# Experts placed by their row count with a capacity per place; gate and up with the weights held still

## What is computed

```python
eidx, gates = _route(xt, router_w, router_bias)      # 6 of 64 experts for each row, and their weights
...
def step(acc, blk):                                  # a block: rows tok of one expert e, gates g
    tok, g, e = blk
    xb = xpad[tok]
    hid = jax.nn.silu(xb @ w_gate[e]) * (xb @ w_up[e])   # (rows, 1024) @ (1024, 256), twice
    yb = (hid @ w_down[e]) * g[:, None]                  # (rows, 256) @ (256, 1024)
    return acc.at[tok].add(yb.astype(acc.dtype)), None
```

## Time and profile before

| what | value |
|---|---|
| median of 3 runs | 2303.5 us (2300.52 to 2303.54) |
| the profiled execution, its own time | 2310.06 us |
| its span in the trace | 2307.7 us |
| TensorE, busy share of the span | 94% |
| VectorE, ScalarE, GpSimd | 61%, 49%, 28% |
| granted TensorE clock, mean | 0.97 |
| first and last matmul of the experts stage | 1028.4 us and 2236.0 us |

### The profile page before, as it was taken

One profiled execution on the slowest core, in us unless ns is written; L12 is line 12 of the kernel. 1 busy time (PEld: TensorE's weight loads), 2 busy tenths in 40 slices (PEclk: granted clock), 3 DMA queues, 4 the chain that ended last, 5 costly groups with the idle time before them and its releaser, 6 DMA issues. The chain is left out here.

```text
span 2307.7 us, 34429 instructions
## 1 busy us (share of the span) xinstructions
PE 2164.2 (94%) x10800; PEld 1766.7 (77%) x10800; DVE 1405.2 (61%) x2590; ACT 1129.7 (49%) x1866; POOL 645.4 (28%) x597
## 2 busy tenths in 40 slices
PE   6999999999899999959999999999999999999970
PEld 5777778777678888747888888888888888888850
DVE  5444444444677877746666666666666666666638
ACT  4344334433533333215556565555655565655537
POOL 1111111111113233332333333333333333333310
PEclk9999999999899999969999999999999999999995
DMA  6101101012623323247999989999999998999958
GB/s 218 40 31 34 41 32 37 34 41 84 244 67 107 101 81 109 93 161 224 284 286 279 277 275 285 281 280 281 280 287 284 284 278 276 275 286 280 282 110 323
DMA packets 194561, 435.84 MB, mean 189 GB/s; under 512 B 35488, under 2 KB 40080, under 8 KB 193200
## 3 DMA queue, kind: packets, MB, share of 16 engines
q1 hardware_dynamic: 150928, 289.49, 36.8%
q0 software_dynamic: 43312, 144.90, 23.6%
q10 hardware_dynamic: 288, 1.05, 0.1%
HBM read 328.16 MB, written 109.39 MB: 190 GB/s over the span
## 5 line engine op out<-in xcount | busy, mean ns | idle before, releaser
L1706 PE MATMUL ex_psU<-ex_guh,ex_xh 128*128 128x512 f32 x1024 | 413.8, 404 | 3.7 <-DVE ex_xl L1691 3.7
L1708 PE MATMUL ex_psU<-ex_guh,ex_xl 128*128 128x512 f32 x1024 | 402.6, 393 | 0.0
L1707 PE MATMUL ex_psU<-ex_gul,ex_xh 128*128 128x512 f32 x1024 | 400.5, 391 | 0.0
L1555 POOL DMA_INDIRECT acc_d<-ex_y,ex_use x128 | 206.3, 1612 | 410.1 <-ACT ex_y L1618 348.9
L1708 PEld LDWEIGHTS ex_psU<-ex_guh,ex_xl 128*128 128x128 f32 x1024 | 193.1, 189 | 43.3
L1706 PEld LDWEIGHTS ex_psU<-ex_guh,ex_xh 128*128 128x128 f32 x1024 | 193.3, 189 | 40.7 <-DVE ex_xl L1691 4.3
L1707 PEld LDWEIGHTS ex_psU<-ex_gul,ex_xh 128*128 128x128 f32 x1024 | 193.9, 189 | 37.5
L1577 POOL DMA_INDIRECT ex_xg<-h_d,entries x128 | 199.3, 1557 | 59.2 <-issue 38.1
L1706 PE MATMUL ex_psY<-ex_dnh,ex_hdh 128*128 128x512 f32 x512 | 210.2, 411 | 1.7 <-DVE ex_hdl L1662 1.7
L1618 ACT ACTIVATE ex_y<-ex_psY 128x1024 f32<-128x1024 f32 x128 | 131.3, 1025 | 143.3 <-PE ex_psY L1708 143.3
L1708 PE MATMUL ex_psY<-ex_dnh,ex_hdl 128*128 128x512 f32 x512 | 200.0, 391 | 0.0
(11 more groups left out here) (351 smaller groups left out, 4400.1 us busy)
## 6 DMA issues: line engine op xcount, KB each, us to landing
mi_g_raw<-w_experts SPq DMA_DIRECT2D x96, 1024.0 KB, 11.8
mi_g_place<-w_experts SPq DMA_DIRECT2D x96, 1024.0 KB, 11.8
mi_xr<-xT SPq DMA_DIRECT2D x17, 512.0 KB, 3.5
acc_d<-de_acc SPq DMA_DIRECT2D x17, 512.0 KB, 13.3
h_d<-de_h POOLq DMA_DIRECT2D x17, 512.0 KB
ln_t<-acc_d SPq DMA_DIRECT2D x17, 512.0 KB, 5.8
y<-ln_t SPq DMA_DIRECT2D x17, 512.0 KB, 4.4
de_cr<-cat SPq DMA_DIRECT2D x16, 512.0 KB
```

What stands on the lines that cost most here:

```text
L1555: nc.gpsimd.indirect_dma_start(out=io["acc_d"], out_offset=bass.IndirectOffsetOnAxis(ap=use[:, k, 0:1].bitcast(U32), axis=0), in_=y[:, k, ...
L1706: nc.tensor.matmul(out, lh, rh, start=start, stop=False)
L1707: nc.tensor.matmul(out, lh, rl, start=False, stop=False)
L1708: return nc.tensor.matmul(out, ll, rh, start=False, stop=stop)
```

## The change

1. **Ranks.** At the end of the dense stage the experts get places: experts 0 and 1 keep the first two, the other 62 follow in rising order of their number of rows. This takes one comparison of all counts with all counts, an inverse by a matmul, and two more round trips between TensorE and VectorE. The order stands in `ov`; SyncE reads the expert of each place from there.
2. **Capacities.** A place has its own number of rows n: 256 for the first two, then 10 places of 176, 14 of 192, 10 of 208, 10 of 220, 8 of 236, 10 of 256 (`CLASSES`). An expert with more rows than its place has the rest in further blocks of 256, which still go in pairs after all others. Each class is a hardware loop of its own with its first pair (on GpSimd two) written out. The second tile of a place has n - 128 rows in gather, add, rounding, split and output.
3. **Gate and up.** The weights are held still (128 x 128 blocks, 32 per expert and part) and the rows move. High and low part of the rows lie side by side in `xs`, so the high weight block meets both in one matmul of 2n columns, and the low weight block meets the high rows in one of n columns. The two halves of the result are added: ScalarE copies the second half (`lo`), VectorE adds (`sums`). The result is hidden x rows, as `down` needs it: `hidden_T`, `psH` and their work are gone. The gate of the rows is now the scale of the output copy.
4. **Order.** A step is now an expert: second half of gate/up of e-1, transposes of tile 0 of e, `down` of tile 0 of e-2, transposes of tile 1, `down` of tile 1, first half of gate/up of e. The adds of e-3 stand behind the gathers of e (before: e-2). The weight transfers wait for their own third of `raw[b]` alone, and a partition's part of a transfer is one piece of 8 KB (before four of 2 KB).

The core of the diff:

```diff
+CLASSES = ((1, 6, 176), (6, 13, 192), (13, 18, 208), (18, 23, 220), (23, 27, 236), (27, 32, 256))
+CAPS = [BLK] * 2 + [n for begin, end, n in CLASSES for _ in range(2 * (end - begin))]
...
-            sp.wait_ge(S["blocks_dve"], 3)
+            sp.wait_ge(S["blocks_dve"], 5)
...
-        xh, y = sb("xh", [P, 2, KC, P], F32R), sb("y", [P, 4, D])
+        xs, hdh = sb("xs", [P, KC, 2, BLK], F32R), sb("hdh", [P, 2, FC, BLK], F32R)
+        lo, gu0 = sb("lo", [P, 2, BLK]), sb("gu0", [P, 2, BLK])
-        psX, psU = ps("psX", [P, D]), ps("psU", [P, 2, 2 * FF])
-        psH, psY = ps("psH", [P, FC * P]), ps("psY", [P, D])
+        psX, psU, psY = ps("psX", [P, D]), ps("psU", [P, FC, 2, 2 * BLK]), ps("psY", [P, 2, D // 2])
...
+            pair(0, BLK, BLK, None)
+            before = BLK
+            for begin, end, n in CLASSES:
+                for p in range(begin, begin + peeled):
+                    pair(p, before, n, None)
+                    before = n
+                with eng.Fori(begin + peeled, end) as p:
+                    pair(p, n, n, None)
...
-                    hold(sp, s_split, 12 * p + 6 * b - 6, s_sp_passed)
                     for kind in range(3):
-                        w = io["w_experts"][bass.ds(e, 1), kind].rearrange("o k p n -> (o p) k n")
+                        hold(sp, s_split, 12 * p + 6 * b - 10 + 2 * kind, s_sp_passed)
+                        w = io["w_experts"][bass.ds(e, 1), kind].rearrange("o p n -> (o p) n")
...
+            # ScalarE
+            def pair(p, n1, n, j):
+                for b in range(2):
+                    e, m = 2 * p + b, n if b else n1
+                    copy_lo(e - 1, 0, m)
+                    round_w(p, e, b, (0,))
+                    sigmoid(e - 1, 0, m)
+                    round_w(p, e, b, (1,))
+                    hidden(e - 1, 0, 1 - b, m)
+                    round_w(p, e, b, (2,))
+                    copy_lo(e - 1, 1, m)
+                    round_x(e, 0, n)
+                    sigmoid(e - 1, 1, m)
+                    round_w(p, e, b, (3,))
+                    output(e - 2, b, (0, 1), n1)
+                    round_x(e, 1, n)
+                    hidden(e - 1, 1, 1 - b, m)
+                    output(e - 2, b, (2,), n1)
+                    round_w(p, e, b, (4,))
+                    output(e - 2, b, (3,), n1)
+                    round_w(p, e, b, (5,))
...
+            # VectorE
+                    sums(e - 1, 0, m)
+                    split_w(e, b, (0,))
+                    activate(e - 1, 0, m)
+                    split_w(e, b, (1,))
+                    hidden(e - 1, 0, 1 - b, m)
+                    sums(e - 1, 1, m)
+                    split_x(e, 0, n)
+                    activate(e - 1, 1, m)
+                    split_w(e, b, (2,))
+                    split_x(e, 1, n)
+                    split_w(e, b, (3,))
+                    hidden(e - 1, 1, 1 - b, m)
+                    split_w(e, b, (4, 5))
...
+            def transpose_x(p, e, b, t):
+                pe.wait_ge(s_row[2 * b + t], 16 * (p + 1))
+                after(pe, s_xl, 2 * e + t)
...
+            def gate_up(e, b, f, n):
+                if f == 0:
+                    pe.wait_ge(s_xl, 2 * e + 2)
+                after(pe, s_sum, 2 * e + f - 1)
+                for half in range(2):
+                    c0 = half * FF + f * P
+                    for kc in range(KC):
...
+                        nc.tensor.matmul(psU[:, f, half, 0:2 * n].rearrange("p (s n) -> p s n", s=2), guh[:, b, kc, c0:c0 + P],
+                                         xs[:, kc, :, 0:n], start=(kc == 0), stop=False)
+                        last = nc.tensor.matmul(psU[:, f, half, 0:n], gul[:, b, kc, c0:c0 + P], xs[:, kc, 0, 0:n],
+                                                start=False, stop=(kc == KC - 1))
...
+            def pair(p, n1, n, j):
+                for b in range(2):
+                    e = 2 * p + b
+                    gate_up(e - 1, 1 - b, 1, n if b else n1)
+                    for t in range(2):
+                        transpose_x(p, e, b, t)
+                        down(e - 2, b, t, n1)
+                    gate_up(e, b, 0, n)
```

More of the change, by code:

```diff
@@ L1238, in _ @@
             V.memset(oneb[:], 1.0)
+            V.memset(onesq[:], 1.0)
             V.memset(macc[:], 0.0)
@@ L1505, in piece, with pairs @@
             return src, dnh[:, b, part, :], dnl[:, b, part, :]
[L1507 to L1513, removed]
+        def pairs(eng, pair, peeled=1):
+            more = eng.value_load(ov[0:1, MORE:MORE + 1], min_val=0, max_val=OVP)
+            pair(0, BLK, BLK, None)
[6 more added lines that the diff above has]
+                    pair(p, n, n, None)
             with eng.If(more > 0):
@@ L1580, in pair @@
[L1580 to L1589 removed]
+                            out=xg[0:r, k, :], out_offset=None, in_=io["h_d"],
@@ new lines, in _, with copy_lo, sigmoid @@
+            A = nc.scalar.activation
+            def copy_lo(e, f, n):
+                if exists(e):
+                    act.wait_ge(s_gu, 2 * e + f + 1)
+                    after(act, s_hid, 2 * e + f)
+                    A(lo[:, :, 0:n], psU[:, f, :, n:2 * n], ACT.Copy).then_inc(s_lo, 1)
+            def sigmoid(e, f, n):
+                if exists(e):
+                    act.wait_ge(s_sum, 2 * e + f + 1)
+                    A(lo[:, 0, 0:n], gu[f][:, 0, 0:n], ACT.Sigmoid).then_inc(s_sig, 1)
@@ L1656, in _ @@
+            e = 2 * pairs(act, pair)
+            copy_lo(e - 1, 0, BLK)
+            sigmoid(e - 1, 0, BLK)
+            hidden(e - 1, 0, 1, BLK)
+            copy_lo(e - 1, 1, BLK)
+            sigmoid(e - 1, 1, BLK)
+            output(e - 2, 0, range(2), BLK)
+            hidden(e - 1, 1, 1, BLK)
+            output(e - 2, 0, range(2, 4), BLK)
+            output(e - 1, 1, range(4), BLK)
         @block.vector
@@ L1701, in _ @@
+            e = 2 * pairs(dve, pair)
+            for f in range(FC):
+                sums(e - 1, f, BLK)
+                activate(e - 1, f, BLK)
+                hidden(e - 1, f, 1, BLK)
         @block.tensor
@@ L1728, in down @@
-            def down(m, b, pieces):
-                pe.wait_ge(s_hl, m + 1)
-                pe.wait_ge(s_split, pieces)
-                pe.wait_ge(s_y, m)
-                for hf in range(2):
-                    cols = slice(hf * 512, (hf + 1) * 512)
+            def transpose_x(p, e, b, t):
+                pe.wait_ge(s_row[2 * b + t], 16 * (p + 1))
+                after(pe, s_xl, 2 * e + t)
+                for kc in range(KC):
+                    last = nc.tensor.transpose(psX[:, kc * P:(kc + 1) * P], xg[:, 2 * b + t, kc * P:(kc + 1) * P], ident[:])
+                last.then_inc(s_xT, 1)
@@ L1734, in down @@
+            def down(e, b, t, n):
+                if not exists(e):
+                    return
+                pe.wait_ge(s_hl, 2 * e + 2)
+                pe.wait_ge(s_split, 6 * e + 6)
+                r = rows_of(n, t)
+                for half in range(2):
+                    u = 2 * t + half
+                    after(pe, s_y, 4 * e + u - 1)
                     for f in range(FC):
-                        last = three(psY[:, cols], hdh[:, f, :], hdl[:, f, :], dnh[:, b, f, cols], dnl[:, b, f, cols],
+                        last = three(psY[0:r, half, :], hdh[:, b, f, t * P:t * P + r], hdl[:, b, f, t * P:t * P + r],
+                                     dnh[:, b, f, half * 512:(half + 1) * 512], dnl[:, b, f, half * 512:(half + 1) * 512],
@@ L1760, in _, with pair @@
-            end = pairs(pe, pair)
-            n = 4 * end
-            hidden_T(n - 2, 2)
-            gate_up(n - 1, 3, 1, 12 * end - 2)
-            down(n - 2, 1, 12 * end)
-            hidden_T(n - 1, 3)
-            down(n - 1, 1, 12 * end)
+                    last.then_inc(s_dn, 1)
+            def pair(p, n1, n, j):
+                for b in range(2):
+                    e = 2 * p + b
+                    gate_up(e - 1, 1 - b, 1, n if b else n1)
+                    for t in range(2):
+                        transpose_x(p, e, b, t)
+                        down(e - 2, b, t, n1)
+                    gate_up(e, b, 0, n)
@@ L1770, in stage_norm @@
+            e = 2 * pairs(pe, pair)
+            gate_up(e - 1, 1, 1, BLK)
+            for t in range(2):
+                down(e - 2, 0, t, BLK)
+            for t in range(2):
+                down(e - 1, 1, t, BLK)
 def stage_norm(nc, io):
```

319 lines of the change are left out of this document (139 added, 180 removed).

## The result

The changed kernel takes 2498.8 us (median of 4 runs, 2494.8 to 2500.0) against 2302.6 in the same comparison: 1.085 of the time, 95% interval 1.083 to 1.087. The forecast was 2219 us, faster; the kernel is 196 us slower, and outside the range.

The account below looks back on a forecast made before the run. TensorE was taken as the bound: its expert stretch falls from 1207.6 to 1117.7 us (-90), +4.3 behind it and +1 at the start give -84.6, so 2303.5 becomes 2219 us; range 2190 to 2262.

Parts of the forecast that it names:

- Transfers: Weights, rows, entries and gathers per expert: 4.90 MB in a mean 17.2 us, POOL's extra copy hidden, cost 0.
- the other side: Gate/up rival: short float32r matmuls run like plain float32, 150 to 500 us more, 2370 to 2720 us; chance 0.07.
- my 0.117 us: Gate/up: price of each n-column matmul for all n, between 0.109 for 128-column transposes and 0.1235 for 256 columns.
- the first rival: Gate/up: short matmuls cost their columns alone, the load hides fully; 25 us less, 2194 us; chance 0.10.
- its 0.109: Spacing in us of 128-column transposes in the earlier trace, used as evidence that the block load's time shows.
- the narrow cover of 0.2 us: `psX` free 3.36 to 3.4 us after tile 0's transposes start; transposes and down last 3.61, so no stall.
- the rival of the `psX` chain: Tile 1 transposes: the 0.2 us cover is lost, say 0.5 us per expert late; +32 us, 2251; chance 0.13.
- The five handovers: Ends of the class loops: five more without the read of `more` and branch, 0 to 7 us, taken as 1.
- Transfers did not decide: Rival: rate stays at 281 GB/s, transfers take 1116 us against 1098; +15 to 18 us, 2235; chance 0.05.
- further blocks: Rival: capacities too small, pairs of blocks follow at 37 us each, 2256 us with one pair; chance 0.03.
- The fill: Start of the experts stage: two tiles pass before the first gate/up, 8.6 us at half clock against 4.3 before.
- the ranking: Start: some ten small VectorE operations and two round trips beside idle TensorE; delay 0 to 4 us, taken as 1.

Follow-up runs that it names:

- Experiments 1 and 3: Changed kernel, drain replaced by a semaphore wait: 2229.2 us; changed kernel, former-adds wait, row-number copy and drain moved ahead of the same expert's gathers: 2233.2 us.
- experiment 6: Changed kernel with capacities 220 and 236 made 224 and 240: with the drain 2447.2 us, with a semaphore in its place 2211.4 us.
- experiment 9: Changed kernel with semaphore for drain: capacity 218 for 220, 236 kept, 2215.8 us; 224 and 234 for 220 and 236, 2329.5 us.
- experiment 11: Changed kernel with semaphore and capacities 224 and 240, weights back in four pieces of 2 KB instead of one of 8 KB: 2211.3 us.
- experiment 2: Kernel before the change with a GpSimd drain added in front of each expert's adds: 2311.8 us, ratio 1.0033.
- the 256 case: Changed kernel with every capacity 256: with the drain 2419.2 us, with a semaphore in place of the drain 2303.0 us.

## Why the prediction was wrong

**The step that failed** is in "Transfers": "POOL, busy for 28%, gets one more small copy per expert, hidden. Cost 0." The copy is hidden; the drain behind it was not priced at all. It stands behind the gathers and lasts until they have landed, so it puts their 10 us between the entries and the adds. The forecast followed entries and gathers from the copy to the landing, and never closed them into a loop with the adds and the next copy. That loop is 12 to 13 us without the drain, an estimate from the durations of its parts; with it, it measured 21, above TensorE's 16 to 18. Experiments 1 and 3 show it from two sides: the drain replaced (-270 us), the drain kept and moved (-266). That "SyncE's entries for e still wait for POOL's copy of e-2" stood in the forecast as harmless; it is the link by which the drain reaches TensorE.

**The second omission** is the number of rows in a transfer. I priced capacities by columns and bytes. 92 rows on 4 DMA engines cost some 52 us with the drain and 18 without (experiment 6, which also changes 108 rows to 112; experiment 9 shows that 108 could stay).

**The mechanism of "the other side"** that I had priced, short float32r matmuls at the rate of plain float32, did not occur, though its 2370 to 2720 us hold the measured time. The matmuls of n columns cost less than my 0.117 us at small n: 0.079 at 176, 0.088 at 192, 0.094 at 208, 0.117 at 256; those of 2n columns more, 0.192 against 0.162 at 176. So the first rival, short matmuls by columns alone, was about right for the short one (0.089 at 176 by its price) and wrong in its sum, since the long one took more. A pair at 176, 192 and 208: 0.271, 0.285, 0.300 against 0.279, 0.2925, 0.306 forecast. Gate/up in all 629 us against 636. In the Trainium skill, "TensorE: Matmul & The Clock Gate", section "LDWEIGHTS (loading the stationary operand)", loading a block of 128 columns is put at 107 ns, which the forecast set beside its 0.109. The 0.079 us from the start of a short matmul to the next start is less than that; two such loads, 0.213 us as an estimate by that figure, fit into every pair measured here.

**What held**, read in the kernel of experiment 6 with the semaphore: from first transpose to last matmul 1112.6 us (1020.4 to 2133.0), forecast 1117.7. Steps of 15.93, 16.36, 16.9, 17.3, 17.8 and 18.4 to 18.65 us, forecast 16.2 to 18.3. The transposes of tile 1 start 3.64 us after those of tile 0, no stall: the narrow cover of 0.2 us sufficed, and the rival of the `psX` chain did not occur. The five handovers between the loops add nothing to the steps. Transfers did not decide (experiment 11), though their share was not below 0.92 as forecast but 0.97 at 287 GB/s. No further blocks ran: 128 gathers. The fill is two tiles long as said:

```profile
1020.38 1.97 PE L1776 MATMUL ex_psX<-ex_ident,ex_xg 128*128 128x128 f32 x8 [14.07 <-DMA ex_xg<-h_d,entries]
1024.82 1.94 PE L1776 MATMUL ex_psX<-ex_ident,ex_xg 128*128 128x128 f32 x8 [2.46 <-DVE ex_xs L1737]
1029.13 0.79 PE L1790 MATMUL ex_psU<-ex_xs,ex_guh 128*128 128x512 f32 x1 [2.37 <-DVE ex_xs L1737]
```

8.75 us to the first gate/up (forecast 8.6). The norm began at 2150.5, 17.5 us after the last matmul (forecast 16.1). The first transposes start at 1020.4, not 1 us later than the 1028.4 of the earlier trace rows. With the kernel before and a drain (experiment 2) they start at 1021.9, so the profiled execution of before was probably late there by some 6 us, which would account for the 6.6 us that it stood over its median. In the profiled executions of the changed kernel and its variants that start lies between 1017.9 and 1025.9 us; within this spread the ranking costs nothing that can be seen. Sum for that kernel: forecast 2219, measured 2211.4.

**Left open:** why gathers land sooner with capacities of 256, where the changed kernel with its drain gains 80 us and from rounding to 16 only 52; and whether the 256 case would be quicker in either of its two forms at other row counts.

## What to carry to other kernels

A wait that stands for "all my own work is visible" can also wait for transfers that the engine has issued, as the drain did here for gathers: look at what is in flight in front of it, and price it as their landing time; a semaphore on the one instruction, or a place ahead of the transfers, costs next to nothing here. An engine that is idle three quarters of the time can set the pace through a loop of latencies: add up the loop (here entries, gathers, drain, adds, copy) and compare it with the step of the engine that should decide, above all when the step gets shorter. When sizes become free to choose, price them on every engine that meets them; 220 was cheaper than 224 in columns and dearer in transfers.

## What the runs showed of the hardware

- A drain on GpSimd behind indirect gathers ended 0.20 to 0.37 us after the last of them had landed (61 of 64 cases, and 62 of 64 in experiment 2); with no gather in flight it took 0.67 us in the median.
- An indirect add went over the largest divisor up to 16 of its number of rows: 92 rows over 4 (12.0 us to landing), 96 over 16 (5.5), 106 over 2 (29), 108 over 12 (7.2), 44 and 60 rows over 11 and 15 (5.2 and 4.8). Small transfers of the other queue are late with them: 2 KB of entries 9.4 us instead of 3.7.
- Float32r matmuls with fewer than 256 moving columns got shorter with their columns: 0.079 us at 176, 0.100 at 224, 0.117 at 256, each beside one of twice the columns. The pair did so less than its columns: 0.271 us at 176 and 0.349 at 256, where the columns alone, at 2.4 GHz, are 0.220 and 0.320.
- Waiting for rows, TensorE lost clock too: 0.87 to 0.91 granted in the three windows shown of the changed kernel, 1.00 and 0.98 in those with the semaphore.
